# Moving V products, weight subtractions and two waits in a hybrid retention, dilated and sliding-window trunk

## The reference, cut to what matters

```python
h = rmsnorm(x, norm_mix[0])
rq, rk, rv, rg, dq, dk, dv = split(h @ w_in)      # retention and dilated heads share a projection
ra = silu(rg) * groupnorm(retention(rope(rq), rope(rk) * dk**-0.5, rv))
da = dilated_attention(rope(rmsnorm(dq)), rope(rmsnorm(dk)), dv)   # windows (128,1), (512,4), (2048,16)
x = x + concat(ra, da) @ w_out
x = x + square(relu(rmsnorm(x) @ w_up0)) @ w_down0

q, k, v = split(rmsnorm(x) @ w_qkv + b_qkv)       # 16 query heads, 4 key heads
x = x + banded_attn(rope(rmsnorm(q)), rope(rmsnorm(k)), v, 127, sinks) @ w_out1
x = x + square(relu(rmsnorm(x) @ w_up1)) @ w_down1
```

## Time and profile before

| what | value |
| --- | --- |
| median of three runs | 2323.6 us |
| profiled execution, own time | 2324.3 us |
| its span | 2322.6 us |
| PE busy | 2255.9 us (97%) |
| DVE busy | 1448.6 us (62%) |
| POOL busy | 1102.3 us (47%) |
| ACT busy | 834.1 us (36%) |
| granted TensorE clock, mean | 0.998 |

### The profile page before, as it was taken

The page is one execution under the profiler, slowest core; times in us unless marked ns, Lnnn a source line. Parts: engine busy times, 40 slices in busy tenths (PEclk is TensorE's granted clock), DMA queues, the critical chain, the costliest instruction groups (busy, mean ns, idle before and its releaser), DMA issues.

```text
span 2322.6 us, 35554 instructions
## 1 busy us (share of the span) xinstructions
PE 2255.9 (97%) x12808; PEld 1903.0 (82%) x12808; DVE 1448.6 (62%) x2766; ACT 834.1 (36%) x1733; POOL 1102.3 (47%) x994
## 2 busy tenths in 40 slices
PE   6999999999999999999999899999999999999999
PEld 5787878789978888888887788889978888888887
DVE  6665656472476676577574677772486667577664
ACT  5525252531332233223232455551333223223220
POOL 5323332322284666567465634422275557467561
PEclk9999999999999999999999999999999999999999
DMA  4111111122102110210203111013211210211211
GB/s 130 28 28 29 28 29 28 29 73 87 55 19 73 64 61 21 72 54 18 81 27 113 52 32 32 22 58 96 64 50 33 72 54 18 72 55 36 71 37 73
DMA packets 140984, 120.41 MB, mean 52 GB/s; under 512 B 26048, under 2 KB 126912, under 8 KB 140864
## 3 DMA queue, kind: packets, MB, share of 16 engines
q1 hardware_dynamic: 133488, 103.70, 14.6%
q10 hardware_dynamic: 7376, 15.12, 1.9%
HBM read 110.41 MB, written 8.39 MB: 51 GB/s over the span
## 4 chain that ended last, share of the span: by engine, by line
PE 84%; DVE 8%; issue 3%; POOL 2%; ACT 2%; DMA 1%; SPq 0%; DVEq 0%; ACTq 0%; POOLq 0%
PE gp L498 14%; PE gp L500 13%; PE gp L499 13%; PE sc L500 6%; PE sc L498 6%; PE sc L499 6%; PE tp L499 3%; PE tp L498 3%; PE tp L500 2%; PE tp L567 2%; DVE QK L1507 1%; PE qt L499 1%; PE o_ps L499 1%; PE qt L498 1%; PE o_ps L498 1%
## 5 line engine op out<-in xcount | busy, mean ns | idle before, releaser
L498 PE MATMUL gp<-W_hi,hT_hi 128*128 128x384 f32 (+1 forms) x1152 | 411.4, 357 | 5.7 <-POOL W_lo L1881 5.7
L500 PE MATMUL gp<-W_hi,hT_lo 128*128 128x384 f32 (+1 forms) x1152 | 383.5, 333 | 0.0
L499 PE MATMUL gp<-W_lo,hT_hi 128*128 128x384 f32 (+1 forms) x1152 | 382.4, 332 | 0.0
L2006 POOL TENSOR_TENSOR W_lo<-af,W_hi 128x512 fp32r<-128x512 f32 x168 | 237.0, 1411 | 283.0 <-ACT W_hi L1158 283.0
L1986 POOL TENSOR_TENSOR W_lo<-raw,W_hi 128x1024 fp32r<-128x1024 f32 x72 | 187.4, 2607 | 230.0 <-ACT W_hi L1100 217.1
L1700 DVE TENSOR_TENSOR af<-af 128x512 f32<-128x512 f32 x112 | 81.3, 726 | 300.6 <-ACT af L1141 300.6
L498 PEld LDWEIGHTS gp<-W_hi,hT_hi 128*128 128x128 f32 x1152 | 219.1, 190 | 39.3 <-issue 30.9
L2006 POOL TENSOR_TENSOR W_lo<-rb,W_hi 128x512 fp32r<-128x512 f32 x168 | 242.7, 1445 | 0.0
L499 PEld LDWEIGHTS gp<-W_lo,hT_hi 128*128 128x128 f32 x1152 | 219.3, 190 | 0.0
L500 PEld LDWEIGHTS gp<-W_hi,hT_lo 128*128 128x128 f32 x1152 | 218.4, 190 | 0.0
L498 PE MATMUL gp<-hT_hi,W_hi 128*128 128x512 f32 x512 | 199.5, 390 | 0.0
(11 more groups left out here) (304 smaller groups left out, 5099.0 us busy)
## 6 DMA issues: line engine op xcount, KB each, us to landing
raw<-in_mlp_w_up SPq DMA_DIRECT2D x64, 512.0 KB, 4.1
rb<-in_mlp_w_down SPq DMA_DIRECT2D x56, 512.0 KB, 5.3
raw<-in_hyb_w_in SPq DMA_DIRECT2D x74, 128.0 KB, 2.5
X<-in_x SPq DMA_DIRECT2D x8, 512.0 KB, 7.8
X<-in_x ACTq DMA_DIRECT2D x8, 512.0 KB, 3.5
raw<-in_mlp_w_down SPq DMA_DIRECT2D x8, 512.0 KB, 3.5
raw<-in_swa_w_qkv SPq DMA_DIRECT2D x16, 256.0 KB, 3.1
x_spill<-X ACTq DMA_DIRECT2D x8, 512.0 KB, 2.6
```

Of the source, the lines that this page charges most:

```text
L498: mm(o, a[0], b[0], start=first, stop=False)
L499: mm(o, a[0], b[1], start=False, stop=False)
L500: return mm(o, a[1], b[0], start=False, stop=last)
L2006: E.tensor_tensor(WF_lo[:, c], x(k), WF_hi[:, c].bitcast(f32), ALU.subtract).then_inc(op_ready, 1)
```

## The change

Five edits; in the diff, the line that begins with @@ names the engine and function.

- **TensorE, dilated stage.** The V products of tile a < 4 move from block 1 of slot a + 3 to block 0 of slot a + 4. Their turn back moves from block 0 to block 1 of slot a + 4. The wait on `o_evac` before the transposes of q and k asks for the tile one before the one it asked for, and stands in slots 5 to 8.
- **ScalarE.** The copy of the V product follows: block 0 of slot a + 4, ahead of the copy of the probabilities.
- **VectorE, dilated stage.** `heads_outputs` of tiles 0 to 3 moves from block 1 of slot a + 4 to block 0 of slot a + 5, first of all steps there, and waits for k's copy of tile a + 3. The first `ret_rope` of a group moves ahead of tile 7's first minima.
- **GpSimd, dilated stage.** The splits in slots 6 and 7 wait for the minima of tiles 4 and 5 (`max_ready`).
- **Sliding-window stage.** The 16 splits in the slots go from GpSimd to VectorE, one slot later, between `outputs` and `sums`.

```diff
@@ PE, dr_slots
-                            if in_part(t - 4 + j, 1 - j):
-                                part_values(g, t - 4 + j, 1 - j)
+                            if j == 0 and 0 <= t - 4 < T:
+                                part_values(g, t - 4, int(t - 4 >= 4))
+                            if j == 1 and 4 <= t - 3 < T:
+                                part_values(g, t - 3, 0)
...
-                            if j == (t - 4 >= 4) and 0 <= t - 4 < T:
+                            if j == 1 and 0 <= t - 5 and t - 1 < T:
+                                pe.wait_ge(o_evac, g * T + t - 4)
+                            if j == 1 and 0 <= t - 4 < T:
                                 part_back(g, t - 4)
                             if j == 1 and 0 <= t - 1 < T:
-                                if 0 <= t - 4 < 4:
-                                    pe.wait_ge(o_evac, g * T + t - 3)
                                 heads_T("D", t - 1, g * T)
@@ ACT, dr_slots
+                            if j == 0 and 0 <= t - 4 < 4:
+                                part_copy_O(g, t - 4)
                             if in_part(t - 3, j):
                                 part_probs_T(g, t - 3, j)
                             if in_part(t - 2, j) and j == (t - 2 >= 4):
                                 heads_probs(g, t - 2)
-                            if j == 1 and 0 <= t - 3 < 4:
-                                part_copy_O(g, t - 3)
@@ DVE, heads_outputs
-                if a == 4:
-                    dve.wait_ge(qkt_ready, (g + 1) * T)
+                if a <= 4:
+                    dve.wait_ge(qkt_ready, g * T + min(a + 4, T))
@@ DVE, dr_slots
-                            if j == 1 and 0 <= t - 4 < 4:
-                                heads_outputs(g, t - 4)
-                            if j == 0 and 4 <= t - 5 < T:
+                            if j == 0 and 0 <= t - 5 < T:
                                 heads_outputs(g, t - 5)
...
+                            if j == 0 and r == 0:
+                                ret_rope(g, 0, g * T, n0 + t + GEMM_BANKS)
                             if in_part(t - 2, j):
                                 part_maxima(g, t - 2, j)
                             if j == 0 and 0 <= t - 1 < T:
                                 prep("D", t - 1, a0)
-                            if j == 0 and 0 <= r < T:
+                            if j == 0 and 1 <= r < T:
                                 ret_rope(g, r, g * T + r, n0 + t + GEMM_BANKS)
@@ DVE, sliding-window stage
+            def split_lo(piece, p, slot):
+                dve.wait_ge(w_hi, piece + p + 1)
+                c = slice(2 * W * p, 2 * W * (p + 1))
+                E.tensor_tensor(W_lo[:, slot, c], raw[:, p % 2, 0:2 * W], W_hi[:, slot, c].bitcast(f32),
+                                ALU.subtract).then_inc(w_ready, 1)
...
+                    if 1 <= t <= NG * T and (t - 1) % T in SPLIT_AT:
+                        c = (t - 1) // T
+                        split_lo(P_S + 4 * (c + 1), SPLIT_AT[(t - 1) % T], 1 - c % 2)
                     if 0 <= t - 1 < NG * T:
                         sums("S", t - 1, A_S)
@@ POOL, dr_slots
                         if t in D_SPLIT_AT:
+                            if 4 <= t - 2 < T:
+                                pool.wait_ge(max_ready, g * 4 + t - 5)
                             split_lo(P_DR + 8 * g + 4 * (t // T + 1), D_SPLIT_AT[t], 1 - t // T, 2 * W)
@@ POOL, s_slots
-                    if t < NG * T and t % T in SPLIT_AT:
-                        split_lo(P_S + 4 * (t // T + 1), SPLIT_AT[t % T], 1 - t // T % 2, 2 * W)
```

## The result

The changed kernel takes 2290.9 us, the median of four runs (2289.0 to 2292.3), against 2323.7 for the kernel before (four runs, 2323.4 to 2324.9). The ratio is 0.9856 [0.984, 0.9871]. The forecast was 2295 with a range of 2291 to 2304: the median lies 4 us under the number and 0.1 us under the range. The profiled execution took 2292.3 us where before's took 2324.3, a gain of 32.0 against a forecast of 29.2.

The account below looks back on a forecast made before the run. TensorE was taken to set the time nearly everywhere, so its waits were what could be won. Gains of 16.3 + 6.4 + 4.0 + 2.5 = 29.2 us from the profiled 2324.3 gave 2295.1, written as 2295, range 2291 to 2304.

Parts of the forecast that it names:

- The cause: Sliding-window stage: GpSimd's W_lo subtraction holds VectorE's 128x2 subtraction (1.82 us against 0.16), so TensorE stalls before q/k transposes.
- 19.3 - 2.1 - 0.5 - 0.4 = 16.3: Sliding-window gain in us: TensorE's stalls before q/k transposes, less slot 1, what stays in slot 3, and its neighbour.
- part 1: Sliding-window splits go from GpSimd to VectorE: gain 16.3 us, price taken as 0, range 0 to 3.
- the rule weighed in the prediction: Two-SBUF-input VectorE and SBUF-reading GpSimd instructions share a lock both ways; the new subtraction could hold GpSimd about 1 us.
- 0.6 + 0.59: Sliding-window slots: cover in us behind VectorE's new subtraction, 0.6 before anything shows, then TensorE's 0.59 on top.
- Part 2: GpSimd's splits in dilated slots 6 and 7 wait for VectorE's minima: gain 6.4 of 6.8 us, range 0 to 6.8.
- about even: Dilated stage, before tile 4's probability transposes: ScalarE's exponents and TensorE's arrival were expected to be about level.
- Part 3: Retention's first rotation ahead of tile 7's minima: four stalls of 1.0 go, gain 4.0 us, range 2 to 4.1.
- Part 4: Dilated V products of tiles 0 to 3 in the next slot: saved block ends, 0.63 per group, 2.5 us, range 0 to 3.
- A: Rival: the dilated stage gives little, as ScalarE's copies wait for the moved products; 2304.7 us, chance 0.14.
- B: Rival: the sliding-window collision is moved, not removed, and half that stage's gain is lost; 2303 us, chance 0.11.
- C: Rival: ScalarE becomes the bound in dilated slots 4 to 7; 2335 us at 2.5 per slot, chance 0.03.

Follow-up runs that it names:

- experiment 10: The kernel before, with GpSimd's sliding-window subtraction replaced by a memset of the same tile: 2301.0 us.
- experiment 11: The kernel before, with GpSimd's sliding-window subtraction replaced by a copy of the raw weights: 2308.3 us.
- experiment 3: The kernel before, with only retention's first rotation moved ahead of tile 7's first minima: 2318.0 us.
- experiment 12: The changed kernel, with the last two GpSimd subtractions of the first sliding-window weight block moved behind the gain products of tiles 4 and 6: 2288.4 us.
- experiment 2: The changed kernel, with the 16 sliding-window splits back on GpSimd: 2310.5 us, ratio 0.9934.
- experiment 4: The kernel before, with only GpSimd's splits in dilated slots 6 and 7 waiting for the minima: 2316.3 us.
- experiment 5: The kernel before, with only the V products of tiles 0 to 3, their copies, turns back and outputs moved: 2316.0 us.
- experiment 6: The changed kernel without GpSimd's wait for the minima in dilated slots 6 and 7: 2292.6 us.
- experiment 1: The kernel before, with only the 16 sliding-window splits moved from GpSimd to VectorE: 2303.4 us, ratio 0.9912.
- experiment 9: The changed kernel, with VectorE's first hT_lo subtraction ahead of its last angle operations: 2291.1 us, ratio 0.986.
- experiment 8: The changed kernel, with VectorE's sliding-window subtraction done three times: 2317.0 us.

## Why the forecast was right, and its size not

**The cause** was named rightly: 19.2 us come back with the sliding-window part alone, and experiments 10 and 11 show that it is GpSimd's reading of SBUF, not its being busy.

**The step that failed** is the term "19.3 - 2.1 - 0.5 - 0.4 = 16.3" of part 1, which took each stall as long as its matmul row says. By the slots it is 19.65. The largest miss is in the reading: each stall is some 0.2 longer than its row. In the slot of the earlier trace rows, where nothing stalls, the record ahead of the transposes is

```profile
1478.89 0.38 PE L603 MATMUL o_ps<-ident,Pm 128*128 128x128 f32 x2
```

It ends at 1479.27, and the transposes start at 1479.11, 0.16 before that. A stall is counted only from the end of the record ahead, so this overlap is lost from it. Thirteen stalls have 13.3 in the matmul rows, and their slots got 16.1 shorter: 2.8 us.

The rest is the clock. In slots 2 and 4 of the first group, the term and what was gained lie apart for a reason that the prediction did not look at. First the granted clock in a stretch before slot 4 of the profile before, then the stall of that slot on the weight loads, and the same stall in experiment 3, which has the same code there and a clock of 1.00:

```profile
1318.10:1321.40 3.30, 3.26 (x11) 3.26 (x12) 1.64 (x7) 2.10 (x9) 1.06 (x2) 0.50 0.35 98
```
```profile
1327.04 0.20 PEld L651 LDWEIGHTS qt<-ident,QK 128*128 128x128 f32 x2 [0.29 <-DVE QK L1524]
```
```profile
1320.70 0.44 PE L651 MATMUL qt<-ident,QK 128*128 128x128 f32 x2 [1.41 <-DVE QK L1524]
```

At 0.50 (the level of 1.2 GHz) a projection matmul starts every 0.32 us instead of every 0.17. TensorE came late to slot 4, and the stall there shrank to 0.29. It has no row among the matmuls, so the term has nothing for it, and the slot gained 1.74. Slot 2 is the opposite. In the profile after it has such a stretch:

```profile
1291.50:1294.80 3.30, 3.30 (x16) 2.64 (x14) 0.49 (x1) 0.82 (x2) 1.39 (x3) 0.50 0.00 0
```

It gained nothing (-0.07), where the term has 1.3 and where experiments 10 and 12, without such a stretch in the stage, show 1.4. All other split slots got shorter by 0.96 to 1.89. Without either stretch the stage would have gained some 20.9, by an estimate (the 21.1 of experiment 10, less the 0.2 that slot 4 took longer before than it did in experiments 2 to 5). The sum of the weight loads, 23.6 before less 3.8 after, is 19.8 and looks like the 19.65, but partly by luck: it has 1.5 for slot 2, which gained nothing, and nearly nothing for slot 4, which gained 1.74.

**The range** was too narrow on that side. The prediction gave each other part an upper bound, and took this term as read. The median lies only 0.1 us outside, less than two runs of one kernel differ; the 3.3 us of the term are the miss.

**Part 1, the price.** Nothing, as forecast, though closer than forecast. The subtraction takes 0.96 with nothing of GpSimd beside it, as forecast, and 1.12 beside the gain product and the copy of V. The lock works both ways, as the rule weighed in the prediction has it, and the copy of V pays for it too (0.24 to 0.96). The margin measured is 0.4, where 0.6 + 0.59 stood. A weight block of twice the size would have cost time.

**Part 2** was right in what it removes: tile 5's stall is gone. But its cause is shared. By experiments 5 and 6 the moved products alone send the split out of the way in groups 1 to 3, and the wait adds 1.5 us to them. The prediction took the products in slot 7 for a delay of TensorE, and did not see that they delay the split. Before tile 4's transposes, where it said "about even", 0.51 stay in group 1 and about 0.15 in the others. And a stall that was not there before stands in slot 9 of the first and the last group, behind ScalarE's exponents of tile 6:

```profile
96.34 0.71 PE L567 MATMUL tp<-ident,Pm 64*128 64x64 f32 x16 [0.46 <-ACT Pm L988]
```

Experiment 5 has it too, so it comes with the moved products; why only in these two groups is open. By the slots the three dilated parts together give 13.1 against 12.9; with 4.0 and 2.5 for parts 3 and 4 that leaves 6.6 for part 2's 6.4. The split of this sum is the forecast's, not shown: alone, each part gives another number.

**Part 3** was right in the place, and its bound of 4.1 was too low: the step is 1.16 to 1.19 in each group when alone, 4.7 in all, of which 0.34 came back. Within the change it is 0.84, 1.18, 1.19 and 0.83, 4.0; in the first and the last group the stall of part 2 in slot 9 takes the difference.

**Part 4** by its own formula was right. For the slots of one group it asks for +0.58, +0.43, +0.43, +0.22 and -1.03 (blocks that leave or enter each slot); group 1 shows +0.62, +0.46, +0.45, +0.28 and -1.22. What it did not foresee is that the same move puts off GpSimd's split (experiment 5).

**The rivals.** A (the dilated stage gives little) is refuted by 13.2 us in experiment 2; what it feared, that ScalarE waits for the moved products, does happen (1.50 at 196.06), and it is what sends the split out of the way. B (the collision is moved, not removed) by 19.2 in experiment 1; its mechanism is real, but it holds GpSimd where GpSimd has time. C (ScalarE becomes the bound) by ScalarE's idle 1.33 before the exponents at 200.54, for which it waited on VectorE; in slots 4 to 7 of every group ScalarE is idle for 2.2 us or more from one slot's transposes to the next.

## What to carry to other kernels

A tiny VectorE operation with two SBUF operands that takes as long as a GpSimd operation beside it is the sign of this lock; move the long one to where VectorE has nothing of that kind, or onto VectorE itself, and count the margin behind it first. Read the size of TensorE's stalls from the distance between like slots, or from the weight loads, not from the matmul rows; and look at the granted clock of each slot that you compare, for a stretch of half clock can swallow a stall or stand in for one. Parts of a change that act on the same stall don't add; what one is worth within the change is found by taking it out, not by doing it alone. And look where the operation that collided went: here a move on TensorE shifted one on GpSimd, by way of ScalarE.

## What was not expected of the hardware

**The lock at the start.** In the profile after, three of VectorE's angle operations lie under GpSimd's first splits, which began at 11.98 (13.45 before):

```profile
12.25 1.98 DVE L1387 TENSOR_TENSOR nn<-nn,ang 128x320 f32<-128x320 f32 x1
14.27 1.81 DVE L1389 TENSOR_SCALAR nn<-nn 128x320 f32<-128x320 f32 x1
16.00 1.88 DVE L1392 TENSOR_SCALAR gainD<-gainD 128x128 f32<-128x128 f32 x1
```

Before they took 0.49, 0.33 and 0.22. Two of them have one tensor operand, so it isn't two-operand operations alone that are held. The section of the Trainium skill named above lists `tensor_scalar` among the operations that can enter a mode with both ports, when their operands allow it, and so contend; the rows agree. The code there is the same; only the weights landed at another moment. What it costs can be read beside the other profiles. All kernels but that of experiment 9 have the same code up to slot 2 of the first group. Its q and k transposes start at 49.7 us in the profile after and in experiment 11, each with three operations held, and at 46.4 to 47.0 in eight profiles with at most one held. That is some 3 us. In experiment 2, which has the same dilated stage and no operation held, that stage ends 2.6 us further ahead of before's than in the profile after.

**Spread between executions.** Executions of one and the same kernel differ by 3 us and more (2289.0 to 2292.3 for the changed one, 2305.4 to 2311.2 in experiment 2). The traces show two things that differ where the code is the same. One is the lock at the start. The other is where the granted clock is at 0.50, the level of 1.2 GHz: in the profile before from 34.7 to 38.0, 44.9 to 48.2 and 1318.1 to 1321.4 us, in the profile after from 45.7 to 48.9 and 1291.5 to 1294.8. From 1314 to 1318 us, ahead of one of them, TensorE had been busy for 2.0 us of 4; from 1287 to 1290, ahead of another, for 1.0 of 3. Three profiles (before, experiments 8 and 12) have two such stretches ahead of that slot 2 and start its transposes at 48.3 to 48.7, some 2 us after the eight named above, which have one; in experiment 12 two operations are held as well. Where TensorE would have stalled anyway a stretch costs little: the one at 1318.1 cost 0.2. That these two make the whole spread is an inference from one profile of each kernel, and was not tested by itself.
